# Gated delta layer: the state's part is taken from the scaled values before the inverse is applied, in place of a product of the inverse with the scaled keys

## The reference, cut to what matters

```
A = where(strict, (k * beta) @ k.T * decay, 0)
uw = solve(A + I, [v * beta, k * beta * exp(gc)])      # u and w
def step(S, inp):
    v_new = u_n - w_n @ S
    o = qd_n @ S + qk_n @ v_new
    S = S * gl_n + kd_n.T @ v_new
```

## Time and profile before

| what | value |
|---|---|
| time, median of three runs | 2094.81 us (2090.91 to 2095.06) |
| time of the profiled execution | 2092.24 us |
| its span | 2090.5 us |
| PE busy | 2037.8 us, 97% of the span |
| PE weight loads | 1758.1 us, 84% |
| DVE busy | 1432.9 us, 69% |
| ACT busy | 976.9 us, 47% |
| mean granted TensorE clock | 0.992 |

### The profile page before, as it was taken

How to read it: one execution, slowest core, us unless ns; L and a number is a source line. 1 busy time by engine, 2 the same in 40 slices (tenths; PEclk the granted TensorE clock), 3 DMA queues, 4 the chain that set the end, 5 groups by cost and what they waited for, 6 DMA issues and landing times. The chain is left out here.

```text
span 2090.5 us, 37167 instructions
## 1 busy us (share of the span) xinstructions
PE 2037.8 (97%) x14961; PEld 1758.1 (84%) x14961; DVE 1432.9 (69%) x2785; ACT 976.9 (47%) x1877; POOL 129.8 (6%) x121
## 2 busy tenths in 40 slices
PE   8999999999999999999999999999999999899997
PEld 8997777899988877779999887878887888688886
DVE  5347865988865677589887457666666766685566
ACT  5337972555400266545552005444444544465454
POOL 1113330000000400000000002000000000020000
PEclk9999999999999999999999999999999999899998
DMA  5230001233232211023333231221112111121211
GB/s 186 83 140 21 2 2 61 91 111 112 92 121 95 98 70 54 29 73 102 111 102 123 89 110 41 81 82 51 51 66 73 60 60 61 38 82 61 82 41 41
DMA packets 30665, 159.36 MB, mean 76 GB/s; under 512 B 3392, under 2 KB 3904, under 8 KB 17856
## 3 DMA queue, kind: packets, MB, share of 16 engines
q1 hardware_dynamic: 30240, 157.24, 21.5%
q10 hardware_dynamic: 288, 0.20, 0.0%
HBM read 155.33 MB, written 2.10 MB: 75 GB/s over the span
## 5 line engine op out<-in xcount | busy, mean ns | idle before, releaser
L224 PE MATMUL ps<-late_parts,panel_upper 128*128 128x256 f32 (+1 forms) x1376 | 460.7, 335 | 0.0
L223 PE MATMUL ps<-late_parts,panel_upper 128*128 128x256 f32 (+1 forms) x1260 | 434.0, 344 | 2.5 <-issue 1.8
L225 PE MATMUL ps<-late_parts,panel_parts 128*128 128x256 f32 (+1 forms) x1260 | 426.1, 338 | 0.0
L219 DVE TENSOR_TENSOR panel_parts<-panel_sb,panel_upper 128x512 fp32r<-128x512 f32 (+1 forms) x334 | 327.7, 1008 | 14.6 <-ACT panel_upper L731 9.0
L223 PE MATMUL ps<-panel_upper,hT_parts 128*128 128x256 f32 (+2 forms) x964 | 295.5, 307 | 7.5 <-DVE h_lower L926 7.5
L225 PE MATMUL ps<-panel_upper,h_lower 128*128 128x256 f32 (+2 forms) x964 | 283.5, 294 | 0.0
L224 PEld LDWEIGHTS ps<-late_parts,panel_upper 128*128 128x128 f32 x1376 | 260.8, 190 | 25.7 <-issue 0.2
L224 PE MATMUL ps<-panel_parts,hT_parts 128*128 128x256 f32 (+2 forms) x964 | 282.3, 293 | 0.0
L223 PEld LDWEIGHTS ps<-late_parts,panel_upper 128*128 128x128 f32 x1260 | 238.7, 189 | 33.3 <-issue 2.4
L225 PEld LDWEIGHTS ps<-late_parts,panel_parts 128*128 128x128 f32 x1260 | 239.8, 190 | 29.0
L223 PE MATMUL ps<-hT_parts,panel_upper 128*128 128x512 f32 (+1 forms) x508 | 199.9, 394 | 4.2 <-DVE h_lower L3444 2.5
(11 more groups left out here) (540 smaller groups left out, 3731.2 us busy)
## 6 DMA issues: line engine op xcount, KB each, us to landing
panel_sb<-ffn_gate_up_w SPq DMA_DIRECT2D x76, 512.0 KB, 4.4
panel_sb<-gdn_w SPq DMA_DIRECT2D x24, 1024.0 KB, 4.8
panel_sb<-ffn_down_w SPq DMA_DIRECT2D x22, 1024.0 KB, 4.8
panel_sb<-nsa_w SPq DMA_DIRECT2D x13, 1024.0 KB, 5.2
panel_sb<-gla_w SPq DMA_DIRECT2D x12, 1024.0 KB, 5.0
panel_sb<-gdn_out_w SPq DMA_DIRECT2D x8, 1024.0 KB, 4.9
panel_sb<-ffn_gate_up_w SPq DMA_DIRECT2D x6, 1024.0 KB, 4.8
panel_sb<-nsa_out_w SPq DMA_DIRECT2D x4, 1024.0 KB, 4.8
```

Of the source, the lines that this page charges most:

```text
L219: return engine.tensor_tensor(out, src, hi.bitcast(F32), ALU.subtract)
L223: mm(out, w_hi, x_hi, start=start, stop=False, skip_group_check=skip_group_check)
L224: mm(out, w_hi, x_lo, start=False, stop=False, skip_group_check=skip_group_check)
L225: return mm(out, w_lo, x_hi, start=False, stop=stop, skip_group_check=skip_group_check)
```

## The change

U's products with the scaled keys are gone, with `kbeg` and its four copies on ACT, and `nwT` with its copy. In their place ACT makes `k_minus`, the transposed keys negated (one 128x512 operation at the start of the chain). For t of 1 and more PE forms k_minus times the state into a bank of its own (signals g_ks), DVE scales it by beta exp(gc) and adds it into `vb` (signals g_rest), and only then does PE form U times `vb` (signals g_v). The gate steps are dealt out anew over the state loop: step 0 before `key_products`; for t = 0, 1 and 2 one step behind the last product; for t of 1 and more one step before the wait on g_rest and two before the wait on g_vnew. In all it is 13 steps in the loop, where six stood, and three behind it, where ten stood. In the last chain, which has no next head, there are none, before as after.

```diff
-    kbeg, kdec = take(TT, P), take(TT, P)
+    kdec = take(TT, P)
...
-    nwT = take(TT, P)
+    k_minus = take(T)
...
+    V_BANK = (3, 6)
...
+        def gate_steps(h, m0, m1):
+            for m in range(m0, m1):
+                project_gate(h, m // DC, m % DC, m % DC + 1)
...
             pe.wait_ge(S("g_inv"), i * 2 + 2)
-            for t in range(TT):
-                last = mm(ps[:, 7, t * P:(t + 1) * P], kbeg[:, t, :], U[:, t, :], start=True, stop=True)
-            last.then_inc(S("g_wT"), 1)
             pe.wait_ge(S("g_vb"), i + 1)
             for t in range(TT):
-                bank = 3 if t % 2 == 0 else 6
                 tok = slice(t * P, (t + 1) * P)
-                last = mm(ps[:, bank, 0:GDN_DV], U[:, t, :], vb[:, t, :], start=True, stop=t == 0)
-                if t == 1:
-                    pe.wait_ge(S("g_nw"), i + 1)
-                    pe.wait_ge(S("g_qd"), i + 1)
                 if t:
                     pe.wait_ge(S("g_state"), i * (TT - 1) + t)
-                    last = mm(ps[:, bank, 0:GDN_DV], nwT[:, t, :], state, start=False, stop=True)
-                last.then_inc(S("g_v"), 1)
-                if t:
+                    if t == 1:
+                        pe.wait_ge(S("g_kminus"), i + 1)
+                    mm(ps[:, V_BANK[(t - 1) % 2], 0:GDN_DV], k_minus[:, tok], state, start=True, stop=True).then_inc(S("g_ks"), 1)
+                    if t == 1:
+                        pe.wait_ge(S("g_qd"), i + 1)
                     if t >= 2:
                         pe.wait_ge(S("g_osum"), i * TT + t - 1)
                     mm(o_tile(t, h is None), gqd[:, tok], state, start=True, stop=False)
+                    if h is not None:
+                        gate_steps(h, 4 * t - 2, 4 * t - 1)
+                    pe.wait_ge(S("g_rest"), i * (TT - 1) + t)
+                mm(ps[:, V_BANK[t % 2], 0:GDN_DV], U[:, t, :], vb[:, t, :], start=True, stop=True).then_inc(S("g_v"), 1)
                 if h is not None:
-                    project_gate(h, 0, t and 2 + t, 3 + t)
-                    if t == 0:
+                    if t:
+                        gate_steps(h, 4 * t - 1, 4 * t + 1)
+                    else:
+                        gate_steps(h, 0, 1)
                         key_products(h, KK_BANK)
                 pe.wait_ge(S("g_vnew"), i * TT + t + 1)
...
                 mm(o_tile(t, h is None), qk[:, t, :], vnew[t % 2], start=t == 0, stop=True).then_inc(S("g_o"), 1)
+                if h is not None and t < TT - 1:
+                    gate_steps(h, 4 * t + 1, 4 * t + 2)
             if h is not None:
-                project_gate(h, 0, 6, DC)
-                project_gate(h, 1)
+                gate_steps(h, 13, 2 * DC)
                 row_decays(h)
...
             for t in range(TT):
-                nc.scalar.activation(kbeg[:, t, :], ps[:, 7, t * P:(t + 1) * P], ACT.Copy, scale=hbeg[:, t:t + 1])
                 last = nc.scalar.activation(kdec[:, t, :], ps[:, 7, t * P:(t + 1) * P], ACT.Copy, scale=hexp[:, 1, t:t + 1])
-            last.then_inc(S("g_kbeg"), 1)
+            last.then_inc(S("g_kdec"), 1)
+            nc.scalar.activation(k_minus, conv[1], ACT.Copy, scale=-1.0).then_inc(S("g_kminus"), 1)
...
-            act.wait_ge(S("g_wT"), i + 1)
-            nc.scalar.activation(nwT[:, :, :], ps[:, 7, :].rearrange("p (t c) -> p t c", t=TT), ACT.Copy, scale=-1.0).then_inc(S("g_nw"), 1)
...
-            nc.vector.tensor_tensor(hbeg, hcol[:, BETA, :], hexp[:, 0, :], ALU.mult).then_inc(S("g_beg"), 1)
+            link(nc.vector.tensor_tensor(hbeg, hcol[:, BETA, :], hexp[:, 0, :], ALU.mult))
...
             for t in range(TT):
+                if t:
+                    dve.wait_ge(S("g_ks"), i * (TT - 1) + t)
+                    nc.vector.scalar_tensor_tensor(vb[:, t, :], ps[:, V_BANK[(t - 1) % 2], 0:GDN_DV], hbeg[:, t:t + 1], vb[:, t, :], ALU.mult, ALU.add).then_inc(S("g_rest"), 1)
                 dve.wait_ge(S("g_v"), i * TT + t + 1)
-                nc.vector.tensor_copy(vnew[t % 2], ps[:, 3 if t % 2 == 0 else 6, 0:GDN_DV]).then_inc(S("g_vnew"), 1)
+                nc.vector.tensor_copy(vnew[t % 2], ps[:, V_BANK[t % 2], 0:GDN_DV]).then_inc(S("g_vnew"), 1)
```

More of the change, by code:

```diff
@@ L2814, in chain @@
                 if l == 1:
-                    pe.wait_ge(S("g_kbeg"), i + 1)
+                    pe.wait_ge(S("g_kdec"), i + 1)
                 pe.sem_inc(S("waited_apart"))
@@ L2981, in chain @@
             act.wait_ge(S("g_kt"), i + 1)
-            act.wait_ge(S("g_beg"), i + 1)
+            act.wait_ge(S("g_decay"), i * 4 + 4)
             for t in range(TT):
-                nc.scalar.activation(kbeg[:, t, :], ps[:, 7, t * P:(t + 1) * P], ACT.Copy, scale=hbeg[:, t:t + 1])
                 last = nc.scalar.activation(kdec[:, t, :], ps[:, 7, t * P:(t + 1) * P], ACT.Copy, scale=hexp[:, 1, t:t + 1])
-            last.then_inc(S("g_kbeg"), 1)
+            last.then_inc(S("g_kdec"), 1)
+            nc.scalar.activation(k_minus, conv[1], ACT.Copy, scale=-1.0).then_inc(S("g_kminus"), 1)
             if first:
@@ L3334, in dve_gdn @@
         with dve.Fori(1, GH - 1) as i:
-            link.begin(i, 20, 1)
+            link.begin(i, 21, 1)
             chain(i, i - 1, i + 1)
```

## The result

The changed kernel takes 2125.09 us in the median of four runs (2123.7 to 2127.68). The kernel before takes 2094.93 beside it (four runs, 2090.91 to 2095.68). The ratio is 1.0156, 95% interval 1.0143 to 1.0168: 30 us slower. The profiled execution took 2123.7 us, its span is 2121.9. The forecast was 2117, with a range of 2109 to 2129.

The account below looks back on a forecast made before the run. PE and DVE were taken as in balance in the state loop, with PE waiting for DVE's convolution 3 at the key products. Seven chains at 2.8 us plus 2.8 for the last gave 22.4, so 2117 us, range 2109 to 2129.

Parts of the forecast that it names:

- L2874's 0.89 us turn into idle time: At the key products: they still wait for convolution 3, so the 0.89 us of removed products per head wins nothing.
- Two gate steps leave: Ahead of the key products: 0.72 us more idle per head, about 1.86 us in all, and the 0.72 done later.
- the sum: Over the whole kernel: seven chains at 2.8 us plus 2.8 us for the last chain, 22.4 us slower.
- The state loop: In the loop over t: DVE's chain grows to 3.75 us a step from 2.51; last v_new copy 3.65 us later.
- Behind the loop: At the transposes of y: PE waits 1.7 us for y, and the gate projection resumes 2.8 us later per head.
- ACT at nothing: On ACT and the other engines: fewer short copies and one larger operation beside PE, counted as no change in time.
- The last chain, 2.8: In the chain without a next head: links take 11.2 us against 7.53, less 0.89 won, so 2.8 us later.
- the term for the clock: PE's clock at the new stands: the forecast of 2117 added no time for a fall of the clock.
- favoured case: Whole kernel: waits and DVE's chain decide, 2117 us, own range 2110 to 2124; 72%.
- this rival: At the stands before the key products and transposes: four to eight clock falls add 7 to 14 us, 2124 to 2131; 14%.
- PE's work decides: Whole kernel: PE has 0.89 us less per head, 7.1 us faster in all, 2087.7; 6%.
- only the moved gate steps count: In and behind the loop: waits are covered and y is in time, 7.8 us more, 2102.6; 8%.

Follow-up runs that it names:

- both moves: The changed kernel with three gate steps put ahead of the key products and four more ahead of the transposes of y: 2113.94 us, ratio 1.0101.
- two gate steps late: The kernel before, with two of its three gate steps moved from ahead of the key products to behind the first qk product: 2097.37 us, ratio 1.0024.

## Why the prediction was right, and what it missed

1. *L2874's 0.89 us turn into idle time.* Right. The key products start at 1556.38, when convolution 3 ends (1554.01 + 2.32 = 1556.33), and their stand is 1.86 us, as forecast (0.25 + 0.89 + 0.72). The run with the short convolution shows that it is this operation that holds them.

```profile
1554.01 2.32 DVE L3122 SCALAR_TENSOR_TENSOR arena_sb<-ps,arena_sb 128x511 f32<-128x511 f32 x3
```

2. *Two gate steps leave.* Right as to the stand, and 0.72 us per head is their price where PE is the bound (0.70 in the kernel before). But in the changed kernel it isn't part of the sum: with the steps put back the trip stayed 70.13.

3. *The state loop.* Right: period 3.77 for 3.75, links of 1.22, 1.27 and 1.28 for 1.21, 1.27 and 1.27. The new step on DVE costs what L3274 costs.

4. *Behind the loop.* From the copy of the last v_new to y it is 3.46 us as before (3.45), and PE loses 1.8 us there by its waits, 0.24 of which it lost before too, for a forecast of 1.7 more. I put all of it on y; half of it stands at `row_decays`, for the column sums. The sum of the step held: 2.90 us per trip for 2.8.

5. *ACT at nothing.* Right for this kernel. But ACT's way behind y was closer than I had thought, as the runs that covered the wait for y showed.

6. *The last chain, 2.8.* Measured 2.81.

**What was mis-sized is the term for the clock.** The sum took the stand of 1.86 us at its own length, and left the clock at 1.00. It fell in six chains of seven, 1.56 us each, 9.4 us in all, which is about the distance from the sum's 22.4 us to the trace's 32.1. The measured 2125 lies outside the favoured case's own range of 2110 to 2124; it is inside 2109 to 2129 only because that kept most of the clock's case, so the hit on the range is the rival's and not the forecast's. I had named this rival and its price well (a loss of 1.7 us for each fall, 2124 to 2131) and given it 14%. The step that failed was the reason against it: that the new stands are shorter than the two of the earlier trace rows, one of which left the clock alone. Of two such stands one had brought the clock down, which gave no ground to expect it from none of the seven at the key products. Nor was the other a safe counterexample: behind that same stand the clock fell in five of the 13 traces kept, as the last section shows. The stands at the transposes never brought it down.

Where the clock is out of it, the sum holds closely: with the gate steps back, the one execution at a mean clock of 0.993 took 2113.45 us, and those of the kernel before at the same clock beside it 2090.6 to 2091.7, so 22 to 23 us for the sum's 22.4.

The Trainium skill, Perfetto Trace Analysis, section Matmul Optimizations, says that the matmul engine scales its power by its utilization, so that matmuls should run back to back: the trace after agrees in six chains of seven, with 0.57 around the key products, and so do the 8 to 10 us won by useless products.

Against the other rivals: that PE's work decides fell with the wait at L2711, and with it, once more, the rule of the Trainium skill, Perfetto Trace Analysis, section Identifying the Most-Contended Engine, to relieve the engine of the highest occupancy first: PE, at 97%, got 0.89 us less to do per head and the trip grew by 2.9 to 4.5. That only the moved gate steps count fell with the period of the loop.

## What to carry to other kernels

Where a product is moved behind an elementwise step to save another product, count the links between the engines first: each time that a serial loop crosses to DVE and back costs about 1.25 us here, whatever it saves in products, and PE's 97% says nothing on that. Then look at what stood ahead of the place where PE waits anyway. Work taken from there wins nothing, and can cost the clock; if nothing useful fits in, even useless work can pay: here it won 8 to 10 us.

## What the hardware did that I had not expected

- The same stand of 1.9 us (1.92, 1.86) behind the same instructions left the clock at 2.4 GHz in the first chain and brought it to 1.2 GHz in the six others, in the changed kernel and again in the one with the old last chain; in the run with four gate steps ahead of the transposes it fell in five of seven. Stands at the key products of 0.97 to 1.21 us, in four kernels of seven chains each, never did, nor did seven of 1.49 us at the column sums (gate steps back) and six of 1.66 us ahead of the output projection (both moves). So length alone doesn't decide it; what else does was not tried.
- Nor does the code around a stand decide it. In each of the 13 traces kept, PE stands for 2.16 to 2.19 us at about 406 us and again at about 959. The clock fell behind the first in seven of them, the kernel before among them, and behind the second in five. The kernel before and the one with the gate steps back run the same code there:

```profile
956.00:964.00 8.00, 6.02 (x51) 5.82 (x50) 8.00 (x15) 4.63 (x9) 0.00 (x0) 1.00 0.37 131
```

```profile
956.00:964.00 8.00, 6.01 (x39) 5.81 (x38) 8.00 (x15) 4.32 (x9) 0.00 (x0) 0.79 0.38 131
```

- A fall that begins about the end of the stand is paid by the work behind it: the key products took 1.66 us from their first weight load to the next line's in place of 0.89, and the clock was back some 3 us later.
- In three of the runs (gate steps back, both moves, two gate steps late) the clock was 0.60 to 0.66 from 1288 to 1292 us, at a place that none of these edits touches, and 1.00 there in the kernel before. The run with two gate steps late has this fall and the one at 960 more than the kernel before, and comes to its first key products 2.95 us later (1346.10 against 1343.15).
- Much of the spread of 4 us between executions of one kernel goes with this. Of 56 executions of the kernel before, timed beside the experiments, the 33 with a mean granted clock of 0.993 took 2089.4 to 2091.9 us, the 16 with 0.991 took 2093.4 to 2094.8, and the seven with 0.990 or 0.989 took 2094.2 to 2095.9. Where a change leaves the clock alone, runs that differ by 2 to 4 us are best compared at the same mean clock.
